# A MoE router with stationary weights and sorted maxima, single buffers in the expert stages, and two more slots for expert weights

## The reference, cut to what matters

```python
coarse = xf @ wg + bg                      # 4 groups
grp = argmax(coarse); p_grp = softmax(coarse)[grp]
fine = (xf @ we + be)[:, grp]              # 8 experts of the chosen group
top_v, top_i = lax.top_k(fine, 2)
weight = p_grp * softmax(top_v)
# every token goes to its two experts:
y = (silu(x @ w1[e]) * (x @ w3[e])) @ w2[e]
out[token] += weight * y
```

## Time and profile before

| | us |
|---|---|
| median of 3 runs | 1432.27 |
| lowest, highest | 1431.74, 1435.51 |
| the profiled execution | 1444.0 |
| its span, first to last instruction | 1442.2 |
| TensorE busy in the span | 1318.3 (91%) |
| DVE busy | 429.7 (30%) |
| ACT busy | 221.8 (15%) |
| POOL busy | 104.4 (7%) |
| mean DMA rate over the span | 342 GB/s |

### The profile page before, as it was taken

The page is one execution under the profiler, slowest core; times in us unless marked ns, Lnnn a source line. Parts: engine busy times, 40 slices in busy tenths (PEclk is TensorE's granted clock), DMA queues, the critical chain, the costliest instruction groups (busy, mean ns, idle before and its releaser), DMA issues.

```text
span 1442.2 us, 15116 instructions
## 1 busy us (share of the span) xinstructions
PE 1318.3 (91%) x6161; PEld 633.1 (44%) x6161; DVE 429.7 (30%) x887; ACT 221.8 (15%) x461; POOL 104.4 (7%) x127
## 2 busy tenths in 40 slices
PE   5999998899999998999988989889999989999897
PEld 3444466643343333433335446763334333343333
DVE  3474855411121210211114963441211111111012
ACT  2223332211010110101110033111110111011010
POOL 2020003000300300300000000000000000000000
PEclk9899998899999998999998999789999999899998
DMA  9982584189999999999999266228999999999993
GB/s 367 383 255 99 217 353 176 44 341 429 428 429 427 428 428 429 428 426 428 428 422 361 99 226 254 109 79 347 428 427 428 428 427 428 428 429 427 428 428 144
DMA packets 51769, 493.45 MB, mean 342 GB/s; under 512 B 4712, under 2 KB 5936, under 8 KB 20848
## 3 DMA queue, kind: packets, MB, share of 16 engines
q1 hardware_dynamic: 48816, 488.33, 81.7%
q10 hardware_dynamic: 1856, 3.20, 0.6%
q0 software_dynamic: 1024, 0.88, 0.4%
HBM read 489.24 MB, written 3.15 MB: 341 GB/s over the span
## 4 chain that ended last, share of the span: by engine, by line
PE 60%; DMA 27%; DVE 8%; issue 2%; ACT 1%; SPq 1%; DVEq 0%; POOLq 0%; POOL 0%; PEldq 0%; ACTq 0%
PE B L784 26%; DMA ring<-in_moe_w 24%; PE B L801 8%; PE A L811 4%; PE A L701 4%; PE B L613 4%; DMA ring<-in_ada_w 3%; PE B L588 3%; PE B L756 2%; PE B L552 2%; PE B L1044 1%; PE B L629 1%; PE B L728 1%; DVE hT L1164 1%; PE B L541 1%
## 5 line engine op out<-in xcount | busy, mean ns | idle before, releaser
L784 PE MATMUL B<-ring,work 128*64 128x512 f32 x2048 | 488.3, 633 | 37.1 <-DMA ring<-in_moe_w 34.6
L784 PEld LDWEIGHTS B<-ring,work 128*64 128x64 f32 x2048 | 156.0, 143 | 328.8 <-issue 327.4
L801 PE MATMUL B<-ring,work 128*64 128x512 f32 x1024 | 242.1, 617 | 1.2 <-ACT work L1787 1.2
L1396 DVE TENSOR_TENSOR work<-work,B 64x512 f32<-64x512 f32 x64 | 68.1, 1064 | 502.7 <-ACT work L1783 502.3
L801 PEld LDWEIGHTS B<-ring,work 128*64 128x64 f32 x1024 | 75.2, 140 | 147.7 <-issue 147.7
L1783 ACT ACTIVATE work<-B 64x512 f32<-64x512 f32 x64 | 37.7, 589 | 612.5 <-PE B L784 612.5
L811 PE MATMUL A<-work 128*128 128x256 f32 x512 | 122.5, 394 | 8.8 <-DVE work L1402 8.8
L811 PEld LDWEIGHTS A<-work 128*128 128x128 f32 x512 | 95.7, 192 | 31.2 <-issue 17.0
L2031 POOL COPY work<-work 128x512 f32 x62 | 38.2, 616 | 897.0 <-PE B L784 747.2
L1402 DVE COPY work<-B 64x512 f32<-64x512 f32 x64 | 43.7, 684 | 127.8 <-PE B L801 127.8
L1791 ACT COPY work<-B 64x512 f32<-64x512 f32 x64 | 37.2, 582 | 204.9 <-PE B L801 204.9
(11 more groups left out here) (267 smaller groups left out, 918.7 us busy)
## 6 DMA issues: line engine op xcount, KB each, us to landing
ring<-in_moe_w SPq DMA_DIRECT2D x192, 2048.0 KB, 18.7
ring<-in_ada_w SPq DMA_DIRECT2D x24, 2048.0 KB, 15.0
ring<-in_ev_w_in SPq DMA_DIRECT2D x6, 2048.0 KB, 13.2
ring<-in_od_w_in SPq DMA_DIRECT2D x4, 2048.0 KB, 14.5
ring<-in_ev_w_out SPq DMA_DIRECT2D x2, 2048.0 KB, 19.7
ring<-in_od_w_out SPq DMA_DIRECT2D x2, 2048.0 KB, 7.7
s_tables<-hT ACTq DMA_DIRECT2D x8, 256.0 KB, 9.5
ring<-s_tables SPq DMA_DIRECT2D x1, 2048.0 KB, 24.9
```

Source lines behind the costliest of these rows:

```text
L784: ins = pe.matmul(B5[64 * m:64 * m + 64, :], xs[:, k, :], w[:, k, :], start=(k == 0), stop=(k == KD - 1))
L801: ins = pe.matmul(B7[64 * m:64 * m + 64, :], hidTb[:, q % 2, k, :], w[:, k, 512 * m:512 * m + 512], start=(k == 0), stop=(k == KF - 1))
L1396: dve.tensor_tensor(hid[64:128, q % 2, :].rearrange("p (k q) -> p q k", k=KF), silu_a[64:128, q % 2, :].rearrange("p (q k) -> p q k", k=KF ...
```

## The change

- **Two more slots, for expert loads only.** `early`, a tile of one slot's size, takes in `BT`, `CT`, `K0`, `modrow`, `crep` and `s5row`, all used up before the expert stage of layer 1, and is room 7 there. The last 4096 columns of `work` are room 6 in both expert stages; SP waits for the last attention product (`pv_done`) ahead of its first load in each layer, and for the last adaLN transposes ahead of room 7's.
- **Single buffers.** `Sw`, `SwT`, `silu_a`, `hid`, `hidTb` and `y2` have one buffer each, which makes that room. The copy of the transposed combining matrix moves from the first to the second expert of a group, behind a wait for the preceding addition; `Sw` is made by eight DVE instructions of 64 columns for a group, where four of 256 columns stood.
- **The logits.** The router's weights are stationary and hT moves: eight matmuls of 256 columns, four ahead of `token_major(0)` and four after the second half of hT. Even and odd blocks are summed in separate partitions; ACT and DVE copy the two partial sums to `rstd`, and two matmuls with a 0/1 matrix add them and turn them to token-major.
- **The top two.** DVE's sorted maximum of eight and `match_replace` take the place of the two `first_max` searches. The positions come from one maximum and one sum; the experts' weights and the chunk count move behind both halves of the packing matrix.
- **Clearing.** Two of the four output banks are cleared ahead of the rank products and two behind them.

```diff
-    slot, fill, old, last, count = [], [], [], {}, [0] * RING
+    slot, fill, old, last, count = [], [], [], {}, [0] * ROOMS
...
+            rank = {x: used_rank(last[x]) for x in range(RING)}
+            if l is not None:
+                for x in range(RING, RING + 1 + l):
+                    rank[x] = max(last.get(x, -1), N_MOE[l] - 2.5)
+            s = min(rank, key=lambda x: rank[x])
...
+                if slot(n) == RING and old is None:
+                    sp.wait_ge(pv_done, N0 if n < N_MIX1 else N0 + N1)
+                if slot(n) == RING + 1 and old is None:
+                    sp.wait_ge(tr_done, U["ada1c2"] + 1)
...
+                def logit_sum(h):
+                    for k in range(4 * h, 4 * h + 4):
+                        m = k % 2
+                        ins = pe.matmul(B5[64 * m:64 * m + NG + NE, 0:TOK], wge[:, l, k, :], hT[:, k, :],
+                                        start=(k < 2), stop=(k > 5), skip_group_check=True)
+                    return ins
+                pe.wait_ge(h_ready, 2 * (2 * l + 1) + 1)
+                logit_sum(0)
                 token_major(0)
                 pe.wait_ge(h_ready, 2 * (2 * l + 1) + 2)
+                logit_sum(1).then_inc(logit_sums, 1)
+                pe.wait_ge(logit_rows, 2 * l + 2)
                 for t in range(TT):
-                    for k in range(KD):
-                        ins = pe.matmul(B5[:, 36 * t:36 * t + 36], hT[:, k, P * t:P * t + P], wge[:, l, k, :],
-                                        start=(k == 0), stop=(k == KD - 1))
+                    ins = pe.matmul(B5[:, TOK + 36 * t:TOK + 36 * t + 36], rstd[:, P * t:P * t + P], addup[:, :], start=True, stop=True)
                 ins.then_inc(logit_done, 1)
                 token_major(1)
+                clear_outputs(0)
+                clear_outputs(1)
                 pe.wait_ge(mask_ready, l + 1)
...
+                clear_outputs(2)
+                clear_outputs(3)
...
-                first_max(fine, m1, oh)
-                stt(t1, oh, -3.0 * BIG, fine, ALU.mult, ALU.add)
-                first_max(t1, m2, oh2)
-                tt(M, oh, oh2, ALU.add)
+                for t in range(TT):
+                    ins = dve.max(top[:, t, :], fine[:, t, :])
+                link(ins)
+                tt(dif, fine, top[:, :, 0:1].to_broadcast([P, TT, NE]), ALU.subtract)
+                tell(route_d)
+                link(dve.memset(top[:, :, 2:8], -SENT))
+                for t in range(TT):
+                    ins = dve.match_replace(rest[:, t, :], top[:, t, :], fine[:, t, :], SENT)
+                link(ins)
+                ts(M, rest, SENT, None, ALU.is_equal)
                 tell(mask_ready)
...
+                stt(at, lg, 1.0, M, ALU.add, ALU.mult)
+                dve.tensor_reduce(first[:, :, 0], at, AX, ALU.max)
+                link(dve.tensor_reduce(both[:, :, 0], at, AX, ALU.add))
+                stt(second, both, -1.0, first, ALU.add, ALU.subtract)
+                packed_rows(0, first, second)
+                ts(second_hi, second, -float(TOK), None, ALU.add)
+                packed_rows(1, first, second_hi)
...
+                        if j == 1:
+                            if NE * l + GE * G:
+                                dve.wait_ge(main.comb, (NE * l + GE * G) // 2)
+                            copy_dispatched(main, 0, 4, sbase + G)
```

More of the change, by code:

```diff
@@ L43 @@
 RING = 6
+ROOMS = RING + 2
 SLOT = 4096
@@ L73, in stream @@
 def stream():
-    slot, fill, old, last, count = [], [], [], {}, [0] * RING
+    slot, fill, old, last, count = [], [], [], {}, [0] * ROOMS
     for n in range(N_ALL):
-        s = n if n < RING else min(last, key=lambda x: used_rank(last[x]))
+        l = next((l for l in range(LAYERS) if 0 <= n - N_MOE[l] < 3 * 32), None)
+        if n < RING:
+            s = n
+        else:
+            rank = {x: used_rank(last[x]) for x in range(RING)}
[3 more added lines that the diff above has]
+            s = min(rank, key=lambda x: rank[x])
         count[s] += n != S5_AT
@@ L81, in stream @@
         fill.append(count[s])
-        old.append(last.get(s))
+        old.append(last.get(s) if s < RING or last.get(s, -1) >= N_MOE[l] else None)
         last[s] = n
@@ L168, in build @@
         starti = sb("starti", [P, NE], I32)
+        addup = sb("addup", [P, NG + NE])
         WORK = 14336
         work = sb("work", [P, WORK])
+        rooms = [ring[:, x, :] for x in range(RING)] + [work[:, WORK - SLOT:], early[:, :]]
         def C(name):
@@ L490, in load_moe @@
                     n = n_moe(l, e, m)
-                    load(n, ring[:, slot(n), :], (w1, w3, w2)[m][NE * l + e])
+                    load(n, rooms[slot(n)], (w1, w3, w2)[m][NE * l + e])
                 def more_loads(gb, i):
@@ L1286, in route @@
                 L = rt[:, 8:11].rearrange("p a t e -> p (a t e)")[:, 0:72].rearrange("p (t c) -> p t c", t=2)
[L1287 removed]
+                tt(L, B5[:, TOK:TOK + 72].rearrange("p (t c) -> p t c", t=2), bge[:, l, :].unsqueeze(1).to_broadcast([P, TT, 36]), ALU.add)
                 co, fi = L[:, :, 0:NG], L[:, :, NG:]
                 sc = rt[:, 12]
[L1290 removed]
+                mx, k1, first, both, second, second_hi, s2, s4 = (sc[:, :, q:q + 1] for q in range(8))
                 g4, e4 = sc[:, :, 8:12], sc[:, :, 12:16]
```

189 lines of the change are left out of this document (92 added, 97 removed).

## The result

The changed kernel takes **1399.4 us** (median of four runs, 1394.35 to 1400.46), beside 1433.1 for the kernel before on the same chip (1431.74 to 1435.51). The ratio is 0.9756, with a 95% interval from 0.9729 to 0.9784: 35 us off 1433.1, 33.7 by the medians. Forecast were 26.2 us and 1406.1; the result lies inside the range, at the place of the rival called "the clock is kinder" (1398.5). The profiled execution took 1394.35, with a span of 1392.5, and is thus the quickest of the four; a second profile of the same kernel, taken beside later experiments, has a span of 1397.4.

The account below looks back on a forecast made before the run. The prediction took the DMA to set the pace of the expert stages, with TensorE following it. Slots 14.7 us plus router 11.5 made 26.2, taking the median from 1432.3 to 1406.1 us; range 1396 to 1414.

Parts of the forecast that it names:

- the clock is kinder: Rival: denser products ahead of the ranks raise TensorE's clock earlier, and it holds to the packing product; 1398.5 us, chance 0.25.
- The slots: Expert stages: each extra slot saves one load of 4.9 us; 4.9 in layer 0, 9.8 in layer 1, 14.7 together.
- the slots bring little: Rival, expert stages: the idle time returns elsewhere and only the router's gain is left; 1420.8 us, chance 0.10.
- the waits would fall by 5 and 10: Sign of being right: TensorE's DMA waits down by some 5 us in layer 0 and 10 in layer 1.
- The single buffers: Expert stages: no new wait, and the added DVE work lies beside a 7.41 us product; cost nothing.
- waits on ACT or DVE: Sign of being wrong: such waits appearing between gate and down products in the expert stages; no size given.
- The first gate product: Sign of being right: starts at about 269.6 in layer 0, 5.4 us sooner from the router's start in layer 1.
- The router: Both layers, ahead of the first gate product: 6.1 us in layer 0 and 5.4 in layer 1, 11.5 together.
- TensorE now stands in the way: Router, before the mask: transposes and clearing take TensorE 4.1 to 5.4 us against DVE's 3.3; 0.8 to 2.1 lost.
- the top two: Router, DVE's chain to the mask: 3.3 us instead of 5.4, so 2.1 less.
- the first packing product: End of the router: 8.9 us instead of 9.62 and 10.21, gains 0.7 and 1.3; 2.2 and 2.8 if the clock holds.
- The change of column shape: Router on TensorE, logit sums alternating with transposes: charged nothing, though the skill says a tiling change drains the engine.

Follow-up runs that it names:

- c_before: The kernel before, run once more with no edit: 1432.44 us in its one run.
- e1: The changed kernel without its extra slots, six in both layers: 1415.59 us, ratio 0.9858 to the kernel before.
- e3: The changed kernel with the router of before, extra slots and single buffers kept: 1417.71 us, ratio 0.9875 to the kernel before.
- e4: The kernel before with only the single buffers and the moved copy and combining matrix, old router, six slots: 1434.05 us, ratio 0.9993 to the kernel before.
- c_after: The changed kernel, run once more with no edit: 1398.12 us, ratio 0.9746 to the kernel before.
- e8: The changed kernel with expert 0's down product moved ahead, between the first and second quarter of the second packing product: 1398.37 us, ratio 0.9755 to the kernel before.
- e5: The changed kernel with the old logits alone, new top two, order, slots and buffers kept: 1410.95 us, ratio 0.9837 to the kernel before.
- e9: The changed kernel with the experts' weights put back ahead of the packing matrix: 1406.69 us, ratio 0.9793 to the kernel before.
- e10: The changed kernel with expert 1's gate and up products ahead of the last three quarters of the second packing product: 1396.91 us, ratio 0.9722 to the kernel before.

## Why the prediction was right in its mechanism and short in its size

**The slots: right, in reason and in size.** Said were 4.9 in layer 0 and 9.8 in layer 1. S0 is 4.5 shorter against c_before, 4.8 against e1, 5.1 between e3 and e4; S1 8.0, 10.1 and 10.0. The reason held as well: the pace of 428 GB/s and the standstill during the first gate product are the same before and after, and what differs is the number of loads left to move from that product on, 90.15 with six slots and 88.15 with eight in layer 1 (summed over stretches of 10 us): of 96 loads eight had landed by then, as foretold. The rival "the slots bring little" fell. One sign was badly chosen: that the waits would fall by 5 and 10. From c_before to c_after they went from 28.6 to 28.7 in layer 0, no fall at all, and from 26.2 to 20.3 in layer 1. The rest of the shortening is in TensorE's busy time over the stage, 439.8 to 435.2 and 438.0 to 435.9 us for the same number of records: products that ran slower behind a wait, as two of the earlier trace rows did. A stage's length takes in both, the wait alone does not.

**The single buffers: right**, nothing (e4). The sign against them, waits on ACT or DVE, did not show either: all of TensorE's waits in a stage that are not for the DMA come to 6.3 and 6.1 us in c_before and in c_after alike.

The first gate product was foretold for 269.6, 6.1 us earlier than before. It came at 257.4, 18.3 earlier. Of these 10.3 are the router's; the other 8.0 are P, which differs between executions.

**The router: right in what it said of DVE and of the order, short in its size**, and this is the error of the prediction. The terms against the rows of the first profile, all in microseconds; each is the difference of two distances in the timelines before and after, the first counted from the end of the second half of hT:

```
                                         layer 0          layer 1
                                      said  measured   said  measured
hT -> logits at DVE                    3.8    4.6       2.5    2.7
logits -> mask taken by TensorE        0.7    2.3       0.7    2.9
mask taken -> packing product starts   0.9    0.9       0.9    0.3
packing product -> gate product        0.7    2.5       1.3    3.1
sum                                    6.1   10.3       5.4    8.9
```

Against c_before, which has the same clock ceiling as the changed kernel, it is 10.0 and 7.8; the experiments on times give 17 (e3) to 19 (e1 against e4), to within 5 and 3 us. Two terms were mis-sized, both by the clock.

The step *TensorE now stands in the way* failed. It took 1.4 us off the 2.1 of the top two. It had the transposes at 2.0, the price at 1.2 GHz, and the clearing at 2.1 to 3.4. With the clock at 2.4 GHz the transposes took 1.07 in both layers and the two banks 1.95, together a little less than DVE's chain, and TensorE had been idle for 0.61 us when the mask came. So it was in 13 of the 14 routers with the new logits, the new top two and the split clearing; in the 14th, e8's layer 0, the clock was low and the step came true, at 0.9 us, as it did with the old logits in e5. What the step had wrong is the clock, not the order of the work. DVE's part was well priced: 3.2 from the logits to the mask, where 3.3 were said, with 0.29 for two sorted maxima and 0.17 for a replacement.

One reading behind the term was off as well. In the kernel before DVE had the mask 5.0 us behind the logits in both layers (258.97 and 940.37). TensorE took it up at 5.5 and 6.1, without having been idle: it was in the way there, and more so in layer 1, where its clearing took longer than the 4.19 of layer 0:

```profile
936.80 4.79 PE L736 MATMUL A<-cst 128*128 128x128 f32 x32
941.43 0.31 PE L741 MATMUL B<-work,cst 128*128 128x32 f32 x2
```

That makes the 2.9 in layer 1; 0.6 of it comes off the next term again, as DVE had gone on with the experts' weights meanwhile.

The step *the first packing product* took 1.5 us of lost clock as paid, though it had seen that the idle stretch would shrink to about 2 us and had priced the other case at 2.2 and 2.8. The rows it went by, four waits in the expert stage, contradict one another at 2.2 to 2.3 us; at 1.84 the clock held every time. That 1.5 twice, and the 1.4 twice that TensorE was not in the way, are 5.8 of the 7.7 missing; the largest net piece of the rest is 0.8 at the logits of layer 0, whose four products took 1.06 and not 1.8.

So the rival **"the clock is kinder"** came true, with 1398.5 against 1399.4, for the reason it gave: the denser products ahead of the ranks. I gave it 0.25. Against it I had held that every hand-over leaves TensorE idle for a moment. That is so, 1.20, 0.73 and 0.61 us, and the clock stayed up all the same. e9 shows the mechanism alone: 1.24 us more of idle time cost 2.9 and 4.1. In part its figure is luck. From c_before to c_after, routers and stages give 17.8 + 12.5 = 30.3 us, where the rival had 33.8; the agreement in time needs the next term, of which it knew nothing.

**Not in the prediction: M.** The mixer between the stages is 5.9 us shorter than in c_before. A part may belong to the slots: M is 1.3 shorter in e3 than in e4 and 2.6 in c_after than in e1, where two executions of one kernel differ by 1.2 and 1.7. Another part goes with TensorE's earlier start behind the stage, which comes with the new logits (e5: M 6.3 longer). How far the two overlap, the table can't say: e1 has the early start and an M only 1.5 shorter than e4. The change did not aim at that start, and by the jump at the program's end another edit may take it away again: as far as the record goes, this part of the gain is luck.

The change of column shape between sums and transposes, for which nothing was charged, shows nothing again: the first sums (128*36 in the rows) end at 236.56 by the model, and the transposes (128*128) begin at 236.49. The drain that the Trainium skill (TensorEngine Tiling (Array Packing), Tiling Modes, Key Properties) names can't be seen here.

## What to carry to other kernels

Where the DMA sets the pace and stands still for want of a free slot, a slot is worth about one load, in each stage that can fill it in advance; measure it by the stage's length, not by the sum of the waits. Freeing a slot earlier was worth much less in the two orders tried: the order has to bring forward all the frees behind it, or the standstill moves instead of going (e8) or most of the lead is given back (e10). When a chain of small steps on another engine is shortened, price TensorE's work in and behind it at both clocks and ask whether the idle stretch gets short enough for the clock to stay: in e9, 1.24 us more of waiting cost another 1.7 and 2.9 us of clock.

## What the chip showed that I had not expected

- Two executions of the kernel before differ in the highest granted clock of their expert stages, 0.95 and 1.00: 7.41 and 7.09 us for a gate product, 1444.0 and 1432.4 us in all.
- A TensorE that had been idle for 3.08 us lost the clock in all three cases, but not at the same moment: twice within the idle stretch, once some 1.2 us into the full work behind it. The price stands in the row of the next product, not beside the wait.
- Behind an expert stage TensorE resumes either as soon as its operand is there or about 5 us later, with no releaser, and which of the two differs between profiles at a place that the edit did not touch. A difference of 5 us between two kernels of this length has to be looked for at such places before it is put down to the edit.
